# Moving the normalised input of a two-layer encoder kernel from 192 to 384 modulo 2048 bytes in a partition

## The reference

```
for l in range(DEPTH):                        # DEPTH = 2
    h = rmsnorm(x, norm_mix[l])
    p = h @ w_in[l]                           # 2048 -> 4608
    y_b = diff_attention(q, k, v, lam, ...)   # 8 heads, 64-token chunks, ALiBi
    y_a = multiscale_pool(a_in, ...)          # trailing means 2, 4, 8, 16
    y_c = conformer_conv(c_in, ...)           # GLU, causal conv of 31 taps, LayerNorm, swish
    x = x + concat(y_b, y_a, y_c) @ w_out[l]  # 2048 -> 2048
    h = rmsnorm(x, norm_ffn[l])
    gu = h @ w_ffn_in[l]                      # 2048 -> 2 * 5504
    g = causal_dwconv(gu[..., :D_FF], ...)    # 3 taps
    x = x + (silu(g) * gu[..., D_FF:]) @ w_ffn_out[l]   # 5504 -> 2048
return rmsnorm(x, final_norm)
```

## Time and profile before

| | |
|---|---|
| median of 3 runs | 2099.13 us (2098.59 to 2099.27) |
| the profiled execution | 2097.42 us |
| its span (first to last instruction) | 2095.3 us |
| PE busy | 2071.9 us (99%), 11892 matmuls |
| PEld busy | 1810.3 us (86%) |
| DVE busy | 1423.2 us (68%) |
| ACT busy | 1103.8 us (53%) |
| DMA | 187 GB/s mean over the span |

### The profile page before, as it was taken

One profiled execution on the slowest core, in us unless ns is written; L12 is line 12 of the kernel. 1 busy time (PEld: TensorE's weight loads), 2 busy tenths in 40 slices (PEclk: granted clock), 3 DMA queues, 4 the chain that ended last, 5 costly groups with the idle time before them and its releaser, 6 DMA issues.

```text
span 2095.3 us, 33423 instructions
## 1 busy us (share of the span) xinstructions
PE 2071.9 (99%) x11892; PEld 1810.3 (86%) x11892; DVE 1423.2 (68%) x2015; ACT 1103.8 (53%) x1562; POOL 48.7 (2%) x43
## 2 busy tenths in 40 slices
PE   9999999999999999999999999999999999999997
PEld 7888888888888888888888878888888888888886
DVE  7997767666666665555489967676666676655555
ACT  6557645555555554433374685455555555544344
POOL 0001100000000000000000011000000000001110
PEclk9999999999999999999999999999999999999999
DMA  8554355555555655555665544655555655555654
GB/s 284 175 181 151 130 191 182 197 187 198 188 182 189 197 190 192 195 195 180 206 212 192 171 141 141 194 190 189 191 189 180 201 190 191 190 191 196 196 193 147
DMA packets 108220, 391.57 MB, mean 187 GB/s; under 512 B 12144, under 2 KB 12656, under 8 KB 107888
## 3 DMA queue, kind: packets, MB, share of 16 engines
q1 hardware_dynamic: 106128, 384.88, 55.5%
q10 hardware_dynamic: 2016, 5.64, 0.8%
HBM read 388.38 MB, written 2.10 MB: 186 GB/s over the span
## 4 chain that ended last, share of the span: by engine, by line
PE 98%; ACT 1%; DMA 0%; DVE 0%; issue 0%; SPq 0%; DVEq 0%; ACTq 0%
PE bank L1146 60%; PE bank L1149 30%; PE bank L1233 2%; PE bank L1222 1%; PE bank L1224 1%; PE bank L1223 1%; DMA raw<-wstream 0%; ACT whi L383 0%; PE bank L1283 0%; PE bank L1304 0%; ACT gt L470 0%; ACT E L483 0%; ACT x L667 0%; DVE x L1080 0%; ACT qT L522 0%
## 5 line engine op out<-in xcount | busy, mean ns | idle before, releaser
L722 DVE TENSOR_TENSOR wlo<-raw,whi 128x1024 fp32r<-128x1024 f32 x728 | 890.1, 1229 | 607.2 <-ACT whi L383 606.5
L1146 PE MATMUL bank<-xg,whi 128*128 128x512 f32 x3648 | 1138.1, 393 | 2.8 <-DVE xg L697 2.3
L383 ACT ACTIVATE whi<-raw 128x1024 fp32r<-128x1024 f32 x728 | 764.4, 1057 | 705.9 <-PE bank L1149 687.5
L1149 PEld LDWEIGHTS bank<-xg,wlo 128*128 128x128 f32 x3648 | 686.1, 188 | 151.6
L1149 PE MATMUL bank<-xg,wlo 128*128 128x256 f32 x3648 | 720.8, 279 | 0.0
L1146 PEld LDWEIGHTS bank<-xg,whi 128*128 128x128 f32 x3648 | 554.3, 188 | 7.1 <-issue 3.3
L1146 PE MATMUL bank<-hidden,whi 128*128 128x512 f32 x1376 | 427.0, 392 | 0.0
L1149 PEld LDWEIGHTS bank<-hidden,wlo 128*128 128x128 f32 x1376 | 258.4, 188 | 56.8
L1149 PE MATMUL bank<-hidden,wlo 128*128 128x256 f32 x1376 | 271.4, 279 | 0.0
L1146 PEld LDWEIGHTS bank<-hidden,whi 128*128 128x128 f32 x1376 | 208.4, 188 | 0.2 <-DVE wlo L722 0.2
L1146 PE MATMUL bank<-mix,whi 128*128 128x512 f32 x512 | 160.6, 395 | 0.0
(11 more groups left out here) (147 smaller groups left out, 902.9 us busy)
## 6 DMA issues: line engine op xcount, KB each, us to landing
raw<-wstream SPq DMA_DIRECT2D x729, 512.0 KB, 3.4
pw_sb<-pww ACTq DMA_DIRECT2D x2, 1024.0 KB, 6.3
x<-xT ACTq DMA_DIRECT2D x3, 512.0 KB, 8.6
outT<-x SPq DMA_DIRECT2D x3, 512.0 KB, 2.9
x<-xT ACTq DMA_DIRECT2D x2, 256.0 KB, 3.9
raw<-wstream SPq DMA_DIRECT2D x2, 256.0 KB, 5.4
poolw_sb<-poolw ACTq DMA_DIRECT2D x2, 256.0 KB, 6.0
outT<-x SPq DMA_DIRECT2D x2, 256.0 KB, 2.8
```

The lines of the kernel that those rows point to most:

```text
L383: nc.scalar.activation(whi[:, s, :], raw[:, s, :], ACT.Copy).then_inc(hi_ready, 1)
L722: nc.vector.tensor_tensor(wlo[:, s, :], raw[:, s, :], whi[:, s, :], ALU.subtract).then_inc(lo_ready, 1)
L1146: nc.tensor.matmul(ps[bank][:], whi[:, s, blk * P:blk * P + P], mov, start=first, stop=False)
L1149: return nc.tensor.matmul(ps[bank][:, 0:S], wlo[:, s, blk * P:blk * P + P], mov[:, 0:S], start=False, stop=last)
```

## The change

Two filler tiles get other sizes. `offset0`, between `x` and `xg`, grows from 64 to 256 bytes in a partition, and `offset1`, between `xg` and `raw`, shrinks from 1984 to 1792 bytes. The sum of both is 2048 bytes before and after. So `xg` alone moves, by 192 bytes: it begins at 384 modulo 2048 in place of 192. Every other tile keeps its address, and no engine's instructions change but for the address of `xg` in those that read or write it; their order is the same on all five engines.

```diff
         x = sb("x", [P, KC, S])
-        sb("offset0", [P, 16])
+        sb("offset0", [P, 64])
         xg = sb("xg", [P, KC, 2 * S], f32r)
-        sb("offset1", [P, 496])
+        sb("offset1", [P, 448])
         raw = sb("raw", [P, RING, PIECE])
```

## The result

The changed kernel takes 2107.97 us (median of 6 runs, 2104.91 to 2109.54) against 2098.97 us of the kernel before (median of 6 runs, 2097.47 to 2099.27). The ratio is 1.0043, with a 95% interval of 1.003 to 1.0055: slower by 9.0 us. The forecast was slower by 24 us. The profiled execution took 2106.64 us with a span of 2104.5 us, 9.2 us more than the span before.

The account below looks back on a forecast made before the run. TensorE's matmul rate was taken as the bound. Terms of +24.3, 0 and 0 us raised the profiled 2097.4 to 2121.7 us, so the median from 2099.1 to some 2124 us; range 2084 to 2140.

Parts of the forecast that it names:

- What bounds the kernel: TensorE's matmul rate: PE busy 2071.9 of 2095.3 us, no other engine or queue limiting the time.
- Term 1: The 3648 matmul pairs that stream `xg`, now at 384: taken as 24.3 us slower.
- (b): Chosen estimate for pairs streaming `xg`: each of both matmuls pays 3.3 ns more, 24.3 us in all.
- (a): Estimate for pairs streaming `xg` by the values group's time per column: 5.0 ns more a pair, 18.2 us.
- Term 2: The 384 values-group matmuls, with `xg` stationary: at most 1.3 us either way, taken as 0.
- Term 3: ScalarE and VectorE writing `xg` at its new place: bound 6.8 us, taken as 0.
- The period: Any dependence on the distance between TensorE's two operands can only repeat every 512 bytes.
- the faster rival: TensorE's two reads meet in SBUF and 256 modulo 512 is farthest apart: 2075 or 2053 us; chance 0.19.
- No effect: The excess per pair is a fixed property of the fp32r stream: 2099 us, within 4 us; chance 0.31.
- much slower: Meeting of TensorE's two reads costs more at 256 than at 64: above +40 us, giving 2154; chance 0.07.
- the likeliest: Slower through pairs streaming `xg`, between +10 and +40 us, own range 2112 to 2136 us; chance 0.43.
- the window over `hidden`: Sign in the timeline: 100 us where `hidden` is streamed still hold 582 matmuls.

Follow-up runs that it names:

- e7_all192: Kernel before with `xg` and every tile behind it moved by the same 192 bytes, all operand distances kept; 2097.17 us beside 2098.23.
- e8_split: Kernel before without `offset0`: `raw` and `whi` at 64, `wlo` and `xg` at 128, `mix` and `hidden` still at 192; 2129.76 us beside 2098.76.

## Why the prediction went as it did

**What bounds the kernel** was right, and the windows bore it out: the loss is all in TensorE's rate, no wait was added (idle before the wide `xg` matmuls went from 2.8 to 2.0 us), and `mix` and `hidden`, which didn't move, kept 2.760 us.

**Term 1** had the right sign and twice the right size. It took +6.7 ns a pair by (b); the trace shows 27 / 8 = 3.4 ns a pair, 12.3 us in place of 24.3. Even (a), 18.2 us, was too high. The step that failed is the choice of the row: the values group's 233.3 ns were read as the price of a moving operand at a multiple of 128. e7_all192, with `xg`, `mix` and `hidden` all at 384, has 2.760 us; and once `xg` had moved the values group, whose moving operand had not, went to 226.7 ns. The 233.3 ns went with how both operands of that group lie to one another, not with the place that it shared with 384. The true value lies below (a): a price of one kind of matmul does not bound another's, even where engine, type and width agree.

**Term 2** was mis-sized: "384 x -3.3 = -1.3 us, or as much the other way", taken as 0. It was -6.7 ns a matmul, -2.6 us. The bound went wrong because it took for granted that the values group could at best reach the pairs' wide matmul of 230 ns; it reached 226.7.

**Term 3** was right: 0 us of stall was added.

**The period** was stated as 512 bytes from the equal cost of all blocks. That was right as far as it went; the experiments show 256. So what the faster rival calls the farthest that there is, 256 modulo 512, is distance 0. That rival's mechanism, by which both operands starting together is worst, isn't borne out in either case: at distance 0 the pairs are slower than at 64 but quicker than at 96, 160 or 224, and the values group is at its quickest.

**The rivals.** No effect is refuted by 2.787 against 2.760 us. The changed kernel beside e7_all192 and e8_split shows that the rate depends on how the places of both operands stand to one another, by up to 2.6% in all runs of the paired order (2.760 to 2.831 us). The Trainium skill, "TensorE: Matmul & The Clock Gate", section "Step-by-step: what each phase is for", says that the two read ports of TensorE are independent and that loading the next weights takes no read bandwidth from the running matmul. What the prediction drew from it, that the distance can't matter and the time stays at 2099, does not hold for this stream. That both reads meet in SBUF would explain the runs; that they meet there, and in which unit, was not shown. Faster and much slower did not come about; of the distances tried, 48, 72, 80, 96, 160 and 224 would have been close to or beyond the forecast (+18 to +32 us on the `xg` pairs alone).

The range held the time, but the likeliest's own range, 2112 to 2136, did not. The chances had no place for it either: no effect went up to 4 us, slower began at 10, and 9.0 lies between. Of the signs, the window over `hidden` came true (582), that over `xg` had 576 where about 571 were expected, its 8 pairs 2.787 us where 2.80 to 2.82 were. The values groups gave the most telling one: at another figure than 233.3 ns they pointed at the stationary operand or the distance, and so against the reason for which (b) was taken.

## What to carry to other kernels

When TensorE is busy for 99% and the time still moves, count matmuls in a window and take starts many matmuls apart: 576 against 582 in 100 us is the whole of this result, while busy shares are equal. In this kernel's dense fp32r stream the place of the streamed tile relative to the stationary one, modulo 256 bytes, is worth 0.5 to 3% of the rate, and the best distance belongs to one order of the matmuls: it has to be found by trying, for each group with its own order, and found again when the order changes. Look at more than one stage, since one distance can have two rates. If a tile has to be moved, moving its partner by the same amount kept the time here (e7_all192).

## What the hardware showed that was not expected

- A move by 192 bytes of one operand changed two kinds of matmul in opposite directions: pairs that stream it +1.0% (2.760 to 2.787 us), matmuls that have it stationary -2.9% (2.800 to 2.720 us for 12).
- 8 bytes off the best distance cost 2.6% of the rate (72, in `hidden`: 2.831 us a piece against 2.760), 128 bytes off only 0.5% (192, in `xg`: 2.773 us).
- In the other order of the matmuls the same group, at the same places, ran at 2.775 us a piece in layer one and at 2.828 in layer two.
- The best rate is exact. Wherever `xg` or `hidden` lay at distance 64 from both weight tiles in the paired order, ten pieces took 27.60 us, with VectorE busy for 67% or for 51%.
- Totals of the changed kernel scatter more than before (4.6 us over 6 runs, against 1.8). The record's mean granted clocks sort them: 0.995 in the three that took 2109.23 to 2109.54 us, 0.996 in the two at 2106.64 and 2106.71, 0.997 in the one at 2104.91. So the scatter goes with the clock; only one of the six has a trace, which shows where.
